# Two-layer encoder on one core: memory keys of layer 2 made earlier, weights landed by halves, shorter choice of experts, output weights by columns

## What is computed

```python
def reference(x, mem, ...):
    mem_n = rms_norm(mem, mem_norm)
    for i in range(2):
        h = rms_norm(x, norm_mix[i])
        mkv = mem_n @ w_mem_kv[i]              # memory keys (256 columns) and values (256)
        if i == 0:                             # 12 heads of neighbourhood attention
            q, k, v, mq = split(h @ na_w_in)
            mix = neighbourhood_attention(q, k, v, na_rpb)
        else:                                  # 4 heads of gated linear attention, chunks of 64
            mix, mq = gla_mixer(h @ gla_w_in, ...)
        att = memory_attention(mq, mkv)
        x = x + concatenate([mix, att]) @ w_out[i]
        x = x + hierarchical_moe(rms_norm(x, norm_ffn[i]), ...)
    return rms_norm(x, final_norm)

# hierarchical_moe: top-1 of 4 groups, then top-2 of its 8 experts, each
#   (silu(t @ w1[e]) * (t @ w3[e])) @ w2[e],  w1, w3: 1024x512, w2: 512x1024, 32 experts a layer
# gla_chunked: within a chunk, tril((q*exp(b - b_mid)) @ (k*exp(b_mid - b))^T) @ v; between
#   chunks a state S = diag(a) S + k^T v
```

## Time and profile before

| | |
|---|---|
| median of 3 runs | 1174.23 us (1173.82 to 1175.13) |
| the profiled execution, its own time | 1174.4 us |
| its span in the trace | 1172.6 us, 1.8 less |
| TensorE matmul busy | 875.2 us (75%) |
| VectorE, ScalarE, GpSimd busy | 225.5, 181.3, 18.6 us |
| read from memory | 442.16 MB, 378 GB/s over the span |
| chain that ended last | PE 54%, DMA 42%, the rest 4% |

### The profile page before, as it was taken

One profiled execution on the slowest core, in us unless ns is written; L12 is line 12 of the kernel. 1 busy time (PEld: TensorE's weight loads), 2 busy tenths in 40 slices (PEclk: granted clock), 3 DMA queues, 4 the chain that ended last, 5 costly groups with the idle time before them and its releaser, 6 DMA issues.

```text
span 1172.6 us, 11688 instructions
## 1 busy us (share of the span) xinstructions
PE 875.2 (75%) x5138; PEld 411.9 (35%) x5138; DVE 225.5 (19%) x427; ACT 181.3 (15%) x385; POOL 18.6 (2%) x15
## 2 busy tenths in 40 slices
PE   8999998383976465655999999976475656575676
PEld 7678553131522121211358665422121212121222
DVE  2234342010011010100115453311010101110012
ACT  3233221010000000000035521200000000000002
POOL 1400000000000000000000000000000000000000
PEclk9999999686998887877999999988787878777789
DMA  9985679999999999999999737999999999999997
GB/s 342 256 269 241 222 310 428 429 427 428 418 429 427 427 428 428 426 427 429 414 284 330 274 144 274 427 425 427 429 428 428 429 429 426 428 428 428 428 419 259
DMA packets 89769, 444.06 MB, mean 379 GB/s; under 512 B 36080, under 2 KB 54896, under 8 KB 67056
## 3 DMA queue, kind: packets, MB, share of 16 engines
q1 hardware_dynamic: 88992, 442.04, 93.5%
q10 hardware_dynamic: 720, 1.19, 0.3%
HBM read 442.16 MB, written 1.05 MB: 378 GB/s over the span
## 4 chain that ended last, share of the span: by engine, by line
PE 54%; DMA 42%; issue 1%; DVE 1%; ACT 1%; SPq 0%; DVEq 0%
DMA ring<-in_moe_w 40%; PE ps L847 15%; PE ps L851 9%; PE ps L704 5%; PE ps L1015 4%; PE ps L744 4%; PE ps L833 2%; PE ps L820 2%; PE ps L1099 2%; PE ps L752 1%; PE ps L684 1%; PE ps L697 1%; PE ps L1065 1%; PE ps L736 1%; PE ps L717 1%
## 5 line engine op out<-in xcount | busy, mean ns | idle before, releaser
L847 PE MATMUL ps<-ring,work 128*32 128x512 f32 x2032 | 274.9, 665 | 146.8 <-DMA ring<-in_moe_w 138.7
L851 PE MATMUL ps<-ring,work 128*32 128x512 f32 (+1 forms) x1088 | 141.8, 681 | 107.1 <-DMA ring<-in_moe_w 104.4
L847 PEld LDWEIGHTS ps<-ring,work 128*32 128x32 f32 x2032 | 82.1, 120 | 326.7 <-issue 326.4
L851 PEld LDWEIGHTS ps<-ring,work 128*32 128x32 f32 x1088 | 40.1, 127 | 197.7 <-issue 191.0
L1775 DVE TENSOR_TENSOR xres<-xres,ps 128x512 f32<-128x512 f32 (+1 forms) x68 | 44.6, 657 | 282.2 <-PE ps L820 282.1
L833 PE MATMUL ps<-xs,work 128*128 128x512 f32 x112 | 55.1, 638 | 10.0 <-issue 9.3
L820 PE MATMUL ps<-work 128*128 128x512 f32 (+1 forms) x136 | 59.7, 581 | 1.6 <-ACT work L1368 1.6
L1766 DVE TENSOR_TENSOR work<-work,ps 128x512 f32<-128x512 f32 x16 | 11.0, 688 | 253.2 <-PE ps L847 253.2
L704 PE MATMUL ps<-ring 128*128 128x384 f32 x160 | 53.4, 490 | 0.0
L1380 ACT COPY work<-ps 128x512 f32<-128x512 f32 x28 | 16.4, 586 | 217.8 <-PE ps L851 217.8
L1359 ACT COPY work<-ps 128x256 f32<-128x256 f32 x16 | 6.0, 372 | 268.0 <-PE ps L879 268.0
(11 more groups left out here) (254 smaller groups left out, 692.8 us busy)
## 6 DMA issues: line engine op xcount, KB each, us to landing
ring<-in_moe_w SPq DMA_DIRECT2D x187, 2048.0 KB, 31.5
ring<-in_w_out SPq DMA_DIRECT2D x4, 2048.0 KB, 16.6
ring<-in_na_w_in SPq DMA_DIRECT2D x7, 1024.0 KB, 12.2
ring<-in_gla_w_in SPq DMA_DIRECT2D x4, 1536.0 KB, 10.8
ring<-in_moe_w SPq DMA_DIRECT2D x4, 1024.0 KB, 19.6
ring<-in_moe_w SPq DMA_DIRECT2D x8, 512.0 KB, 11.4
ring<-in_na_w_in SPq DMA_DIRECT2D x1, 3072.0 KB, 19.9
ring<-in_na_rpb SPq DMA_DIRECT2D x12, 192.0 KB, 5.7
```

The lines of the kernel that those rows point to most:

```text
L847: return pe.matmul(ps[32 * e:32 * e + 32, 4 + m, :], xsel[:, k, 32 * e:32 * e + 32], w, start=k == 0, stop=k == KC - 1, tile_position=(0, ...
L851: return pe.matmul(ps[32 * e:32 * e + 32, bank, 0:w.shape[-1]], actT[:, j, 32 * e:32 * e + 32], w, start=j == 0, stop=j == 3, tile_positio ...
```

## The change

1. Layer 1's key weights come in two transfers of 4 row blocks each (first half on `ring_in[8]`, second on `ring_in[0]`), and `mem_k(0)` waits for the second only before k = 4. The gain vector of layer 1 no longer stands in front of the first normed columns.
2. Layer 2's keys: their 1 MB of weights is issued in group 0 ahead of the fill for slot 7, into the upper part of `work`; `mem_k(1)` runs in group 0 on PE between the w3 products and the transposes. ACT keeps the result (`keep_k1`) before its sigmoid. At the fourth group only the 1 MB of value weights is loaded, and `mem_v(1)` runs.
3. Choice: the triangle has -1024 on its diagonal and `iotam` is 0 to 31 less 1024, so that DVE compares straight out of PSUM; the copy to `ppos` comes after. `positions1` runs two `keep_warm` products in place of one, and the two ahead of it in `route` are gone.
4. Seam between the layers: the first V weights of layer 2 land in two halves by rows, and PE waits for the second half before k = 4 of tile 0.
5. Layer 2's w_out is split by columns: slot 6 holds columns 0 to 511, slot 4 the others. All of tile 1's first half of columns is done before the second half's last six blocks; slot 6 is let go at `wo_half`.
6. `within(0)`, the products inside chunks of the forward direction, stands ahead of the wait for the last memory probabilities.

```diff
-KVB, WOB, OB, KSTB = (0, 2), ((0, 2), (4, 2)), (2, 0), (0, 1, 7, 6)
+KB, VB, WOB, OB, KSTB = (0, 3), (1, 3), ((0, 2), (4, 2)), (2, 0), (0, 1, 7, 6)
-    c[:, C_TRI:C_TRI + P] = np.triu(np.ones((P, P)), 1)
+    c[:, C_TRI:C_TRI + P] = np.triu(np.ones((P, P)), 1) - CHOSEN * np.eye(P)
-    c[:, C_IOTAM:C_IOTAM + 32] = np.arange(32) - 64
+    c[:, C_IOTAM:C_IOTAM + 32] = np.arange(32) - CHOSEN
+        kw1 = cut(work, KEPT, KC, 256)
+        kTm1_kept = cut(work, 1696, MPAIR, T)
-        wow = [[region(0, 0, D, 4), region(6, 0, D, 4)], [region(6, 0, D, 4), region(4, 0, D, 4)]]
+        wow = [[region(0, 0, D, 4), region(6, 0, D, 4)], [region(6, 0, HALF_D, KC), region(4, 0, HALF_D, KC)]]
# free1
-  ... 6: (ring_used, PRE1 - 1),
+  ... 6: (wo_half, 2),
# sync, experts
-                        sp.dma_start(kvw[1], rows(w_mem_kv[1], 0, 512)).then_inc(ring_in[kv_slot], 16)
+                        sp.dma_start(kvw[1], rows(w_mem_kv[1], 256, 512)).then_inc(ring_in[kv_slot], 16)
...
+                        if l == 0 and g == 0 and main[0].slots[f] == 7:
+                            sp.wait_ge(at_tr, N1)
+                            sp.wait_ge(s_memT, 1)
+                            sp.dma_start(kw1, rows(w_mem_kv[1], 0, 256)).then_inc(ring_in[EXTRA], 16)
# sync, start
-            sp.dma_start(kvw[0][:, :, 0:256], rows(w_mem_kv[0], 0, 256)).then_inc(ring_in[0], 16)
+            for half in range(2):
+                k = slice(4 * half, 4 * half + 4)
+                sp.dma_start(kvw[0][:, k, 0:256], rows(w_mem_kv[0], 0, 256)[:, k, :]).then_inc(ring_in[(8, 0)[half]], 16)
# sync, seam
-            sp.dma_start(vw1[0][:, :, 0:HALF], chunk_rows(win1, MIX, MIX + HALF)).then_inc(ring_in[6], 16)
-            sp.dma_start(vw1[0][:, :, HALF:WIDE], chunk_rows(win1, 3 * MIX, 3 * MIX + 32)).then_inc(ring_in[6], 16)
+            for half in range(2):
+                k, there = slice(4 * half, 4 * half + 4), ring_in[(EXTRA, 6)[half]]
+                sp.dma_start(vw1[0][:, k, 0:HALF], chunk_rows(win1, MIX, MIX + HALF)[:, k, :]).then_inc(there, 16)
+                sp.dma_start(vw1[0][:, k, HALF:WIDE], chunk_rows(win1, 3 * MIX, 3 * MIX + 32)[:, k, :]).then_inc(there, 16)
# tensor, quad, after the w3 products
+                if pick_count is None and l == 0:
+                    mem_k(1)
                 pe.wait_ge(rn.sig.sel_ready, sel_count + 1)
...
+                if pick_count is None and l == 0:
+                    pe.wait_ge(kv_cp, 3 + 1)
                 pe.wait_ge(rn.sig.act_ready, c + 1)
# tensor, experts
-                        mem_kv(1)
-                        pe.wait_ge(kv_cp, 3 + 2)
+                        mem_v(1)
+                        pe.wait_ge(kv_cp, 3 + 3)
# tensor, layer 2
             probs_T(N1 + 1, prob1)
+            pe.wait_ge(q_in, 2)
+            pe.wait_ge(k_in, 2)
...
+            within(0)
             pe.wait_ge(at_oT, N1 + 1)
...
-            within(0)
             within(1)
# scalar
+            def keep_k1():
+
+                act_e.wait_ge(kv_mm, 2)
+                act_e.wait_ge(first.sel_ready, 2)
+                nc.scalar.copy(kTm1_kept.rearrange("p m t -> p (m t)"), ps[:, KB[1], :]).then_inc(kv_cp, 1)
...
             def quad(rn, c, pick_count, pair, n0, halves, last_of=None):
+                if pick_count is None and c == 0:
+                    keep_k1()
# vector, place
-                dve.wait_ge(rt_m, 2 * l + a + 1)
-                link(V.tensor_scalar(t32a[:, a, :], msk[:, a, :], -1000.0, 1000.0, ALU.mult, ALU.add))
                 dve.wait_ge(rt_p, 3 * l + a + 1)
-                link(V.tensor_tensor(ppos[:, a, 0:NE], t32a[:, a, :], ps[:, POSB[l], a * NE:(a + 1) * NE], ALU.add))
-                V.tensor_tensor(sel[:, a], iota.unsqueeze(1).to_broadcast([P, E4, CAP]),
-                                ppos[:, a, 0:E4].unsqueeze(2).to_broadcast([P, E4, CAP]), ALU.is_equal).then_inc(done, 1)
+                at = ps[:, POSB[l], a * NE:(a + 1) * NE]
+                V.tensor_tensor(sel[:, a], iotam.unsqueeze(1).to_broadcast([P, E4, CAP]),
+                                at[:, 0:E4].unsqueeze(2).to_broadcast([P, E4, CAP]), ALU.is_equal).then_inc(done, 1)
+                link(V.tensor_copy(ppos[:, a, 0:NE], at))
```

More of the change, by code:

```diff
@@ L376, in build @@
         landed_wo0 = [(ring_in[0], 32), (ring_in[6], 16)]
-        for slot, n in ((0, 2), (1, 1), (2, 1), (3, 2), (4, 2), (5, 2), (6, 1), (9, 1)):
+        for slot, n in ((0, 2), (1, 1), (2, 1), (3, 2), (4, 2), (5, 2), (6, 1), (8, 1), (9, 1)):
             count[slot] += 16 * n
@@ L668, in transposes, with mem_k @@
                     transpose_tile(i, src, a, NBANK[i][a])
-            def mem_kv(l):
-                w = kvw[l]
+            def mem_k(l):
+                w = kvw[0] if l == 0 else kw1
                 if l == 0:
-                    arrived(landed_kv0)
+                    arrived(landed_kv0[0])
                 else:
-                    slot, there = main[0].fill(0, KV_AT * FILLS)
-                    pe.wait_ge(ring_in[slot], there)
+                    arrived(landed_k1)
                     pe.wait_ge(s_memT, 1)
@@ L692, in mem_kv @@
                     pe.wait_ge(s_memv, 16)
+                else:
+                    slot, there = main[0].fill(0, KV_AT * FILLS)
+                    pe.wait_ge(ring_in[slot], there)
                 for a in range(TT):
@@ L1137, in _, with within @@
             probs_T(N1 + 1, prob1)
+            pe.wait_ge(q_in, 2)
+            pe.wait_ge(k_in, 2)
+            def within(d):
+                for h in range(HG):
+                    for n in range(NCH):
+                        c = slice(h * T + n * CH, h * T + (n + 1) * CH)
+                        r = (n % 2) * 64
+                        t = pe.matmul(ps[r:r + 64, 2 + d, (h * TT + n // 2) * CH:(h * TT + n // 2 + 1) * CH],
+                                      ki[:, d, c], qi[:, d, c], start=True, stop=True)
+                t.then_inc(a_mm, 1)
+            within(0)
             pe.wait_ge(at_oT, N1 + 1)
```

95 lines of the change are left out of this document (48 added, 47 removed).

## The result

The changed kernel took 1168.61 us (median of 5 runs, 1167.07 to 1168.80) beside 1174.35 for the kernel before (5 runs, 1173.82 to 1175.45). The ratio is 0.9944, with a 95% interval of 0.9933 to 0.9955: 0.56% or 5.7 us less. I had said 1166.4, with 1163.8 to 1170.4. The profiled execution of the change took 1167.07 with a span of 1165.3, so profile against profile the gain is 7.3 us (1174.4 less 1167.07), and median against median 5.7.

A forecast was written before the change was run, and what follows sets the result against it. PE was taken to bound the mixers and DMA the closed expert streams. Gains of 1.2 + 1.05, 1.9, seam 0.6, chunks 1.0 and layer 2's stream 2.05 made 7.8 us: 1166.6 profiled, 1166.4 median, range 1163.8 to 1170.4.

The forecast's parts named there:

- rival A: Whole kernel: the sum of the terms holds as it stands, 1166.4 us; chance 0.70.
- the term for layer 2's stream: Layer 2's expert stream: 1.0 us from w_out by columns plus 1.05 from the earlier choice, together 2.05.
- my three signs of being wrong: DMA idle near 205; layer 1's last landing moving by other than 4.1; the fill behind the first slice still queuing.
- the bounds of the parts: Lowest and highest gain given for each part; said to total 3.5 all low and 9.3 all high.
- Start: Layer 1's memory keys by halves: PE starts at about 8.45 instead of 9.67, gain 1.2 us, bounds 0 and 1.6.
- Choice: Choice of experts: one product fewer ahead and one DVE step fewer, gain 1.05 us per layer, bounds 0.2 and 1.3.
- the filling product: Choice of experts: with one idle PE product fewer ahead, PE is ready at about the mask's time, 0.86 us gained.
- Keys of layer 2: Keys' 1 MB free in the DMA gap; fourth group's transfer 3.0 instead of 4.9 us, gain 1.9, bounds 0 and 2.45.
- Time in the first group: Layer 1's first expert group: 12.5 us between products, w2 ends at 194.9, limit 199.9; cost 0, 5 us to spare.
- rival C: First group lets the stream run dry: w2 products at half clock take 7.07 more, 2.1 lost, 1168.5 us; chance 0.10.
- Seam: Between the layers: V weights in halves gain 0.6 us, bounds 0 and 0.64; V products start 4.8 earlier (4.15 and 0.6).
- Chunks: Layer 2's mixer: products within chunks fill PE's 1.19 us wait for ACT's copy, gain 1.0, bounds 0.5 and 1.19.

The follow-up runs named there:

- the eleven kernels that are alike there: Experiment kernels mostly identical to the change up to the fill of 132.51, which was issued 0.3 us later in their mean than in the change's profile.
- experiment 12: The changed kernel with layer 1's key weights in one transfer at the start and both engines waiting for both gains, as before: 1171.35 us.
- experiment 7: The changed kernel with the filling products in both layers' choice as before, two ahead of the counting product and one behind: 1168.86 us.
- experiment 2: The changed kernel with the fourth group's transfer again bringing all 2 MB of layer 2's memory weights, the keys' half unused: 1169.76 us.
- Experiment 6: The changed kernel with the product of layer 2's memory keys done twice in the first group: 1173.10 us.
- experiment 5: The changed kernel with ScalarE's sigmoid and its table load ahead of the copy of layer 2's keys in the first group: 1166.89 us.
- kernel 1: The changed kernel with layer 2's w_out by rows again and tile 1's products in their old order: 1168.62 us.
- Experiment 4: The changed kernel with layer 2's first V weights in one piece at the seam, as before: 1168.71 us.
- experiment 8: The changed kernel with the first direction's products within chunks back behind the key transposes: 1169.22 us.
- experiment 9: The changed kernel with the first fill of layer 2's second group held back until the next slice's slot is free too: 1169.25 us.
- the kernels that relieve it: The two changed kernels with the sigmoid ahead of the keys' copy, one also with the V transfer on ScalarE's queue: median 1167.23 us over nine runs.
- the change again: The changed kernel measured again, unaltered: 1168.74 us.

## Why the prediction was right, and where not

The forecast of the profile was 1166.6 and it came to 1167.07: rival A, and most of the gain lies where I had put it. That the two are within 0.5 us is in part luck: the term for layer 2's stream was 1.15 too high and that of the seam 0.6, the V transfer and the end of the span 0.5 each too low. Two of my three signs of being wrong came up: the last landing of layer 1 moved by 4.8 (597.12 to 592.35), not 4.1, and the fill behind the first slice took 9.4, not 8.2. DMA was not idle near 205. Nor do the bounds of the parts add up to the 3.5 and 9.3 that I gave for the range; they make 1.4 and 9.8. Step by step:

- **Start.** 1.2 forecast, 1.23 in the pair of profiles (0.9 against the mean of the eleven kernels that are alike there), 1.3 in experiment 12. The next thing late is DVE's column step, as I had said.
- **Choice.** 1.05 forecast, 1.12 to 1.15 in layer 1, of which 0.85 are the filling product (0.86 forecast; experiment 7 gives 0.85 and 0.86).
- **Keys of layer 2.** The transfer in the gap was free. The V transfer took 2.8 us of the stream, not the 3.0 that I had taken from the start of the kernel: the fill of 259.43 has landed 31.6 after its issue, the V transfer of 259.91 33.9 after its own. (Both it and the old 5.01 have some 0.12 MB of gains and gates in them.) 5.01 less 2.80 is 2.2, and experiment 2 gives 2.2; the other 0.2 of the table's 2.4 were there by the landing of the fill of 176.39. By the Trainium skill (DMA: Bandwidth & Descriptors, Specifications) pieces of this size run at line rate, 2.45 for this megabyte; the trace lies between, nearer to the rule than I had allowed.
- **Time in the first group.** The step was right in its result and its sum was short: 12.5 us forecast between products, and then w2 at full speed, where the clock fell behind the 3.90 us of waiting and added 2.2. That was my rival C, at a third of its price, and it stayed 2.5 us inside the limit. Experiment 6 shows that the limit is where I had it, experiment 5 that it was the wait that brought the clock down. That waits between bursts of products lower the clock is what the Trainium skill (TensorE: Matmul & The Clock Gate, HAM oscillation) says; here 3.90 us did and 2.00 did not, while at the seam and at the end 1.36 to 1.68 did.
- **Seam.** 4.8 forecast, 4.74 measured, but for other reasons than I had given. The stream had gained 4.76 by then and not 4.15, while PE's own path through the last group had gained only 3.9; the wait of 0.64 disappeared and covered the rest. That path scatters by as much as the term: in kernel 1, whose last fill of layer 1 lands 0.3 later, PE's last transposes start 0.55 earlier than in the change (595.07 for 595.62). Experiment 4 gives the halves 0.4 to 0.6, with its fills landing 0.4 later.
- **Chunks.** 1.0 forecast, 0.93 to 1.03 measured, 0.93 by experiment 8.
- **Layer 2's stream: the term that was mis-sized.** I had taken 1.0 + 1.05 from "8.2 is the bare latency". Slot 6 was filled 3.7 us earlier, as I had said, and the fill of the first slice was issued 1.1 earlier, but it landed only 0.9 further ahead than PE was, since it took 9.4 and not 8.2. The 8.2 are those of a fill that finds DMA empty. This one was issued 2.6 us before the fill ahead of it had landed, and most such fills take longer (last section, experiment 9). Why they do stays open.
- **A term left out.** Between the last landing and the end of the span the change is 0.5 us ahead. Before, PE was late there by its own path: it went through the last 32 w2 products without a wait, and the last eight began some 0.6 us behind the landing at 1162.43. In the change PE waits for the landing at 1155.61. PE before, and in the change:

```profile
1161.70 1.93 PE L851 MATMUL ps<-ring,work 128*32 128x256 f32 x32
```

```profile
1155.65 0.64 PE L874 MATMUL ps<-ring,work 128*32 128x256 f32 x8 [0.20 <-DMA ring<-in_moe_w]
```

The rest of the difference to the median stays open. My number was for the median and missed it by 2.2 us; the two profiled executions of the change (1167.07 and 1167.63) are each the fastest of their five, and the others lie at 1167.77 to 1169.27. The second lengths of the seam, 1.6 us, and of the end, 1.3, have the right size; three of the thirteen profiles of changed kernels show one or both. The first group in a slower version would fit too, since the kernels that relieve it are the faster ones. Only profiled executions can be looked into, so neither is shown.

The version with the lowest median is that of experiment 5: 1166.89 us, 7.7 under the 1174.56 of the kernel before beside it.

## What to carry to other kernels

When a stream of transfers is handed over from one stage to the next, count in landings, not in issues: for each late fill take the later of "issue plus latency" and "landing ahead plus transfer", and take the latency from fills that stood the same way to the one ahead. Where a change fills a wait of PE by moving work next to another engine's chain, write that chain out in full, table load and all, because a new wait (3.90 us here) costs its own length and then the clock of the products behind it (2.2 us). An issue that lasts long, or slack that shrinks, costs nothing until the stream opens, so test it by doubling the work in question, as experiment 6 does, before trusting or fearing it.

## What the runs showed of the hardware

**A 2 MB fill that is issued while the one ahead is about to end is mostly slower than one that finds DMA empty.** Over all profiles here, from 125 us on, by how long before the landing of the one ahead the fill was issued:

```
issued ahead of that landing    us from issue to landing
less than 1 us, or after it     7.9 to 8.8
1.0 to 2.0 us                   8.4 to 9.2
2.0 to 4.0 us                   8.0 to 10.7
4 us and more                   4.7 to 5.8 behind the one ahead in 99 of 100 (median 4.9)
```

The medians are 8.2 for the 96 fills of the first row and 9.05 for the 81 of the third; of these the ones issued more than some 3.3 us ahead would queue anyway, by an estimate from 8.2 and the 4.9 of a transfer. The first of the 16 parts in which a fill reports its landing comes 6.5 to 7.2 us after the issue in all cases up to 3 us, so it is the rest of it that is spread out. The same fill of layer 2 took 8.3 (kernel 7), 8.7 (held back, kernel 9), 9.4 (the change), 10.0 (the change again) and 10.4 us (kernel 4); so a handover of this kind carries 2 us of scatter in itself. By estimate, 8.2 less the 4.9 of a transfer in a closed stream leaves 3.3 us for what is not the transfer itself.

**The queue fills by pieces.** With seven fills on their way, a transfer of 1 MB in 1 KB pieces made the next issue on SyncE last 26.71 us (25.04 to 27.37 in the other kernels that have it), one of 2 MB in whole rows 0.43.

**The clock has a price of 1.6 us at the seam and 1.3 at the end**, for waits for DMA that differ little: ahead of the further wait of 0.80, one of 1.09 left the clock at 1.00 at the seam and one of 1.60 did not; at the end 1.26 did and 1.36 did not. The average over the run does not show it (granted clock 0.882 in kernel 12, 0.880 in the change again); the stretch from 562 to 600 us does, with 0.96 for 1.00.
